# Attention of a hybrid block: all four head pairs of a token tile at once, in quarters and column halves of the array

## The reference, cut to what matters

```python
def swa_sink_attention(q, k, v, sinks, cos, sin):
    ...
    s = jnp.einsum('bnqhgd,bnkhd->bnhgqk', q, kb) * (ATT_HEAD_DIM ** -0.5)   # kb: chunk n-1 and chunk n
    s = jnp.where(valid, s, finfo.min)                                      # chunk 0 has none before it
    pr = softmax(concatenate([s, sink], axis=-1))[..., :-1]
    o = jnp.einsum('bnhgqk,bnkhd->bnqhgd', pr, vb)
...
o_b = swa_sink_attention(...)
merged = concatenate([sigmoid(gate_a) * o_a, sigmoid(gate_b) * o_b])
x = x + merged @ w_out[i]
```

## Time and profile before

| | us |
|---|---|
| median of 3 runs | 1765.84 |
| lowest and highest | 1765.23, 1767.95 |
| the profiled execution | 1764.62 |
| its span, first to last instruction | 1762.9 |
| TensorE busy | 1734.0 |
| DVE busy | 1088.1 |
| ACT busy | 905.7 |

### The profile page before, as it was taken

One profiled execution on the slowest core, in us unless ns is written; L12 is line 12 of the kernel. 1 busy time (PEld: TensorE's weight loads), 2 busy tenths in 40 slices (PEclk: granted clock), 3 DMA queues, 4 the chain that ended last, 5 costly groups with the idle time before them and its releaser, 6 DMA issues.

```text
span 1762.9 us, 22796 instructions
## 1 busy us (share of the span) xinstructions
PE 1734.0 (98%) x8277; PEld 1434.9 (81%) x8277; DVE 1088.1 (62%) x1436; ACT 905.7 (51%) x1152; POOL 20.6 (1%) x77
## 2 busy tenths in 40 slices
PE   7999999999999999999999999999999999999996
PEld 6888788888888888888888888888888888888885
DVE  6657776776757766577686454555555555555564
ACT  6556546554555545555456544444444444444453
POOL 4000000000000000000000000000000000000000
PEclk9999999999999999999999999999999999999998
DMA  6655555555655556555556666666666666665553
GB/s 220 200 171 174 148 165 177 159 166 168 190 178 158 166 168 190 178 159 166 168 181 208 186 186 190 191 191 187 193 184 192 189 190 183 193 187 186 174 187 111
DMA packets 162715, 315.32 MB, mean 179 GB/s; under 512 B 10097, under 2 KB 10418, under 8 KB 162482
## 3 DMA queue, kind: packets, MB, share of 16 engines
q1 hardware_dynamic: 161584, 312.01, 58.5%
q10 hardware_dynamic: 1026, 1.87, 0.3%
HBM read 311.74 MB, written 2.10 MB: 178 GB/s over the span
## 4 chain that ended last, share of the span: by engine, by line
PE 96%; DVE 2%; ACT 1%; issue 0%; DMA 0%; SPq 0%; DVEq 0%; ACTq 0%
PE acc L638 30%; PE acc L639 30%; PE acc L644 30%; PE turn L665 2%; PE turn L707 1%; PE turn L683 1%; PE turn L696 1%; DVE w_lo L1218 1%; ACT w_hi L894 1%; PE turn L755 0%; DMA w_raw<-in_w_in_dram 0%; PE turn L728 0%; PE turn L722 0%; DVE x_sb L1295 0%; PE turn L762 0%
## 5 line engine op out<-in xcount | busy, mean ns | idle before, releaser
L1218 DVE TENSOR_TENSOR w_lo<-w_raw,w_hi 128x1024 fp32r<-128x1024 f32 x588 | 720.1, 1225 | 612.4 <-ACT w_hi L894 608.7
L894 ACT ACTIVATE w_hi<-w_raw 128x1024 fp32r<-128x1024 f32 x588 | 623.1, 1060 | 700.8 <-PE acc L644 690.8
L638 PE MATMUL acc<-w_hi,hT_hi 128*128 128x512 f32 x1568 | 624.7, 398 | 6.5 <-ACT w_hi L894 4.0
L639 PE MATMUL acc<-w_hi,hT_lo 128*128 128x512 f32 x1568 | 612.5, 391 | 0.0
L644 PE MATMUL acc<-w_lo,hT_hi 128*128 128x512 f32 x1568 | 419.8, 389 | 0.0
L638 PEld LDWEIGHTS acc<-w_hi,hT_hi 128*128 128x128 f32 x1568 | 295.6, 189 | 68.3 <-ACT w_hi L894 4.4
L639 PEld LDWEIGHTS acc<-w_hi,hT_lo 128*128 128x128 f32 x1568 | 295.8, 189 | 59.9 <-issue 0.4
L644 PEld LDWEIGHTS acc<-w_lo,hT_hi 128*128 128x128 f32 x1568 | 294.3, 188 | 61.7
L638 PE MATMUL acc<-w_hi,mT_hi 128*128 128x512 f32 x512 | 205.5, 401 | 0.0
L639 PE MATMUL acc<-w_hi,mT_lo 128*128 128x512 f32 x512 | 199.7, 390 | 0.0
L644 PE MATMUL acc<-w_lo,mT_hi 128*128 128x512 f32 x512 | 137.3, 390 | 0.0
(11 more groups left out here) (209 smaller groups left out, 898.7 us busy)
## 6 DMA issues: line engine op xcount, KB each, us to landing
w_raw<-in_w_in_dram SPq DMA_DIRECT2D x232, 512.0 KB, 3.7
w_raw<-in_w_up_dram SPq DMA_DIRECT2D x128, 512.0 KB, 3.7
w_raw<-in_w_down_dram SPq DMA_DIRECT2D x128, 512.0 KB, 3.9
w_raw<-in_w_out_dram SPq DMA_DIRECT2D x64, 512.0 KB, 4.5
w_raw<-in_w_ple_gate_dram SPq DMA_DIRECT2D x32, 512.0 KB, 3.9
x_sb<-in_x_dram SPq DMA_DIRECT2D x8, 256.0 KB, 7.8
w_raw<-in_w_ple_proj_dram SPq DMA_DIRECT2D x4, 512.0 KB, 3.9
out_dram<-x_sb SPq DMA_DIRECT2D x3, 512.0 KB, 4.7
```

Of the source, the lines that this page charges most:

```text
L638: pe.matmul(a, hi[:, k, t, :], w_hi[:, s, kk, :], start=first and kk == 0, stop=False)
L639: pe.matmul(a, lo[:, k, t, :], w_hi[:, s, kk, :], start=False, stop=False)
L894: act.activation(w_hi[:, n % W_SLOTS], w_raw[:, n % RAW_SLOTS], ACT.Copy)\
L1218: dve.tensor_tensor(w_lo[:, n % W_SLOTS], w_raw[:, n % RAW_SLOTS], w_hi[:, n % W_SLOTS].bitcast(F32), ALU.subtract).then_inc(w_lo_ready, 1)
```

## The change

The attention of a group goes in two steps, one for each token tile, with all four pairs (8 heads) in each.

- **Scores** (a = 4 and a = 16): 16 matmuls of 128 columns, each on 64 rows (one head of the pair, `hs`) and 64 columns of the array (one chunk of 64 queries, `qs`), so that four matmuls in a row go to the four quarters. The two heads write to two banks (0 and 1). The keys stand in `kTd` unpadded, on both halves of the partitions, and each quarter takes 128 of them.
- **Softmax**: the maximum over all pairs in one go (`parts_of`: for t=0 the first 64 queries have 64 keys, all others 128); the exponentials in four steps, one for each pair, into one tile `pr` with room for 128 keys and the sink, whose exponential ACT writes beside them (16 further instructions a group). A new DVE stage, `weights_normed`, sums, inverts and multiplies, in two halves g, and the transposes wait for it (`pn_ready`).
- **Transposes of the weights**: 4 for each t and g, 16 a group, where there were 24.
- **Values**: the stationary operand is now a 64-column slice of `vv`, the weights stream, and the result is transposed already: for t=0 two matmuls of 512 columns, one to each column half of the array (one head of each pair), for t=1 four of 256 columns. `vv` has a third part with the values of chunks mixed as the third chunk of queries needs them. `weighted_values(j, 0)` stands directly behind the scores of t=1 (a = 16), `weighted_values(j, 1)` at a = 28.
- **Gating**: TensorE transposes the gate (8 transposes at a = 31) in place of the gated result, and DVE multiplies.
- **Once at the start**: 8 transposes of the keys in place of 16; ACT copies half of the values a second time; some clearing by GpSimd is gone.

The attention of a group ends at a = 33, where it ended at a = 44.

```diff
-            kTp = mb("kTp", [P, 4, 2, TT * P])
-            vaug = mb("vaug", [P, TT, 4, HD + 1])
+            kTd = mb("kTd", [P, 4, 5 * CHUNK])
+            vv = mb("vv", [P, 3, 4, HD])
...
-            pr0 = mb("pr0", [P, 2, P])
-            pr1 = mb("pr1", [P, 2, 2 * P])
-            pT = mb("pT", [P, 4, P])
-            oa = mb("oa", [P, TT, 8, HD + 1])
+            pr = mb("pr", [P, 4, 2, P + 1])
+            pT = mb("pT", [P, 2, 4, P])
+            oaT = mb("oaT", [P, 4, TT, P])
...
+        for t in range(TT):
+            use(("kT", t), t, kTd_out, t + 1)
...
-            for u in range(8):
-                use(("score", j, u), 0, pr_ready, 8 * j + u + 1)
-                use(("pT", j, u), 1, pT_out, 8 * j + u + 1)
-                use(("pv", j, u), 1, pv_out, 8 * j + u + 1)
             for t in range(TT):
-                use(("amT", j, t), t, moA_ready, 2 * j + t + 1)
+                for hh in range(2):
+                    use(("score", j, t, hh), hh, pr_ready, 4 * (2 * j + t + 1))
+                for g in range(2):
+                    use(("pT", j, t, g), g, pT_out, 2 * (2 * j + t) + g + 1)
+            use(("pv", j, 1), 0, pv_out, 2 * j + 2)
+            for t in range(TT):
+                use(("gbT", j, t), t, am_ready, 2 * j + t + 1)
...
+                if hp == 0:
+                    use(("pv", j, 0), 2, pv_out, 2 * j + 1)
...
+        SCORES, PV1, ATT_END = (4, 16), 28, 31
...
-            def scores(j, u, t, pair):
-                name = ("score", j, u)
-                if u == 0:
+            def scores(j, t):
+                if t == 0:
                     pe.wait_ge(qaT_out, 2 * (j + 1))
-                    pe.wait_ge(kTp_out, 4)
+                    pe.wait_ge(kTd_out, 2)
+                for hh in range(2):
+                    signal, value = bank_free(("score", j, t, hh))
+                    pe.wait_ge(signal, value)
+                late = kTd[:, j, P:5 * CHUNK].rearrange("p (s c) -> p s c", c=CHUNK)[:, 0:3:2, :]
+                keys = (kTd[:, j, 0:P],) * 2 if t == 0 else (kTd[:, j, P:2 * P], late)
+                for pair in range(4):
+                    for c in range(2):
+                        for hh in range(2):
+                            name, hs = ("score", j, t, hh), slice(hh * HD, (hh + 1) * HD)
+                            qs = slice(c * CHUNK, (c + 1) * CHUNK)
+                            out_ = bank(name)[qs, pair * P:(pair + 1) * P]
+                            if t and c:
+                                out_ = out_.rearrange("p (s c) -> p s c", c=CHUNK)
+                            mm = pe.matmul(out_, qT[hs, pair, t, qs], keys[c][hs], start=True, stop=True,
+                                           skip_group_check=True)
+                            if pair == 3 and c == 1:
+                                mm.then_inc(full(name), 1)
+            def weights_turn(j, t, g):
+                name = ("pT", j, t, g)
+                pe.wait_ge(pn_ready, 2 * (2 * j + t) + g + 1)
...
-                k0, nk = keys_of(t)
-                mm = pe.matmul(bank(name)[:, 0:2 * nk].rearrange("p (v k) -> p v k", v=2),
-                               qT[:, pair, t, :], kTp[:, j, :, k0:k0 + nk], start=True, stop=True)
+                for i in range(4):
+                    hh, pair = i // 2, 2 * g + i % 2
+                    mm = pe.transpose(bank(name)[:, i * P:(i + 1) * P], pr[:, pair, hh, 0:P], ident[:])
                 mm.then_inc(full(name), 1)
-            def weights_turn(j, u, t):
-                name = ("pT", j, u)
-                pe.wait_ge(pr_ready, 8 * j + u + 1)
+            def weighted_values(j, t):
+                name = ("pv", j, t)
+                pe.wait_ge(pT_out, 2 * (2 * j + t + 1))
                 signal, value = bank_free(name)
                 pe.wait_ge(signal, value)
...
-            def weighted_values(j, u, t):
...
+                parts_ = ((0, slice(0, P)),) if t == 0 else ((V_MIXED, slice(0, CHUNK)), (V_LATE, slice(CHUNK, P)))
+                for v, qs in parts_:
+                    for hh in range(2):
+                        mm = pe.matmul(four(bank(name)[hh * HD:(hh + 1) * HD, :])[:, :, qs], vv[:, v, j, :],
+                                       pT[:, hh, :, qs], start=True, stop=True, skip_group_check=True)
                 mm.then_inc(full(name), 1)
...
-                    for i in range(4):
-                        t, half = divmod(i, 2)
+                    for t in range(TT):
                         pe.wait_ge(k_rotated, t + 1)
-                        src = (gate if t == 0 else eg)[:].rearrange("p a b -> p (a b)")
-                        turn(("kT", i), lambda q: src[:, (4 * half + q) * P:(4 * half + q + 1) * P])
+                        turn(("kT", t), lambda i: gate[:, t, i * P:(i + 1) * P])
...
-                    for u in range(8):
-                        t, pair = divmod(u, 4)
-                        if a == UNIT * u + 4:
-                            scores(j, u, t, pair)
-                        if a == UNIT * u + 7:
-                            weights_turn(j, u, t)
-                        if a == UNIT * u + 9:
-                            weighted_values(j, u, t)
-                    if a == ATT_END + 4:
-                        for t in range(TT):
-                            pe.wait_ge(am_ready, 2 * j + t + 1)
-                            turn(("amT", j, t), lambda i: sgb[:, t, i * P:(i + 1) * P])
+                    for t in range(TT):
+                        if a == SCORES[t]:
+                            scores(j, t)
+                            if t == 1:
+                                weighted_values(j, 0)
+                        for g in range(2):
+                            if a == SCORES[t] + 7 + 2 * g:
+                                weights_turn(j, t, g)
+                    if a == PV1:
+                        weighted_values(j, 1)
+                    if a == ATT_END:
+                        for t in range(TT):
+                            pe.wait_ge(gb_sig, 2 * j + t + 1)
+                            turn(("gbT", j, t), lambda i: sgb[:, t, i * P:(i + 1) * P])
...
-            def exponentials(j, u, t, pair):
...
+            def exponentials(j, t, pair):
+                if pair == 0:
                     for hh in range(2):
...
+                        act.wait_ge(full(("score", j, t, hh)), nth(("score", j, t, hh)))
+                    act.wait_ge(nm_ready, 2 * j + t + 1)
+                    act.wait_ge(pr_cleared, j + 1)
+                    if j or t:
+                        act.wait_ge(pT_out, 2 * (2 * j + t))
+                for hh in range(2):
+                    head = t * 8 + 2 * pair + hh
+                    act.activation(pr[:, pair, hh, P:P + 1],
+                                   sink_bc[:, 8 * j + 2 * pair + hh:8 * j + 2 * pair + hh + 1],
+                                   ACT.Exp, bias=asc[:, NM + head:NM + head + 1])
+                    src = bank(("score", j, t, hh))
+                    for rows_, keys in parts_of(t):
+                        ins = act.activation(pr[rows_, pair, hh, 0:keys], src[rows_, pair * P:pair * P + keys], ACT.Exp,
+                                             scale=HD ** -0.5, bias=asc[rows_, NM + head:NM + head + 1])
                 ins.then_inc(pr_ready, 1)
...
-                    for u in range(8):
-                        if a == UNIT * u + 5:
-                            exponentials(j, u, *divmod(u, 4))
+                    for t in range(TT):
+                        for pair in range(4):
+                            if a == SCORES[t] + 2 + pair:
+                                exponentials(j, t, pair)
                     if a == ATT_END + 1:
...
+                        for t in range(TT):
+                            act.wait_ge(am_ready, 2 * j + t + 1)
+                            act.activation(mT_hi[:, 4:8, t, :], four(sgb[:, t]), ACT.Copy).then_inc(moA_hi, 1)
...
-            def score_max(j, u, t, pair):
...
+            def score_max(j, t):
+                for hh in range(2):
+                    name = ("score", j, t, hh)
+                    dve.wait_ge(full(name), nth(name))
+                    for rows_, keys in parts_of(t):
+                        chain(dve.tensor_reduce(asc[rows_, MX + hh:MX + 8:2], four(bank(name)[:])[rows_, :, 0:keys],
+                                                AX_X, ALU.max))
+                if j == 0 and t == 0:
                     dve.wait_ge(sinks_landed, 16)
...
-                dve.tensor_scalar(asc[:, NM + 8 * t + head:NM + 8 * t + head + 2], asc[:, MX:MX + 2], -1.0, None,
+                chain(dve.scalar_tensor_tensor(out=asc[:, MX:MX + 8], in0=asc[:, MX:MX + 8], scalar=HD ** -0.5,
+                                               in1=sink_bc[:, 8 * j:8 * j + 8], op0=ALU.mult, op1=ALU.max))
+                dve.tensor_scalar(asc[:, NM + 8 * t:NM + 8 * t + 8], asc[:, MX:MX + 8], -1.0, None,
                                   ALU.mult).then_inc(nm_ready, 1)
```

(47 more changed lines are left out.)

125 lines of the change are left out of this document (22 added, 103 removed).

## The result

The changed kernel takes 1737.74 us (median of 4 runs, 1736.98 to 1737.94) against 1765.66 for the kernel before (4 runs, 1765.23 to 1767.95). The ratio is 0.984, with a 95% interval of 0.9829 to 0.9852, so the change gains 27.9 us where the forecast had 30.2.

The account below looks back on a forecast made before the run. TensorE, busy 98% of the span, sets the pace. 25.6 us of attention, 0.8 at the start and 3.8 of stall make 30.2: profiled 1764.62 becomes 1734.4, median forecast 1735.6 us, range 1731 to 1746.

Parts of the forecast that it names:

- Four abreast: TensorE's score matmuls run in all four array quarters at once, 0.11 us per pass of 128 columns; chance 0.66.
- the slowest rival: Score passes run one after another, each of 256 with an exposed weight load of at most 0.055 us: 1777.9 us; chance 0.03.
- The visit at 0.37 us: Entering and leaving array tiles on TensorE costs 0.37 us a visit, 4.4 us for twelve; the least sure term.
- Change of shape from scores to values: At a = 16 on TensorE, going from score tiles to value tiles within one visit costs 0.14 us.
- The chunks: TensorE from L644 to L644: a = 4 3.97 us, a = 16 4.99, a = 28 3.97 apart from the recurrence's transposes.
- What is removed and added: TensorE's attention work per group: 13.0 us removed, 6.65 added, 6.4 less, 25.6 in four groups.
- Keys at the start: At the kernel's start TensorE does 8 transposes fewer at 0.105 us each, 0.8 us gained.
- The stall: In group 0 TensorE's wait for DVE's L1375, with the slow clock after it, goes away: 3.8 us gained.
- The waits at nothing: Added waits, such as transposes for `weights_normed` behind work on DVE and ACT, cost TensorE nothing.
- The rival of new waits: Lumps on DVE and ACT make TensorE wait, 3.8 us each: once 1739.4 us, once a group 1750.8; chance 0.10.
- the forecast's own sign: TensorE would show no idle time in the four groups.
- its other sign: TensorE's granted clock would be 1.00 in the four groups.

Follow-up runs that it names:

- b_early: The kernel before with every attention unit started one chunk earlier, nothing else; 1787.95 us, ratio 1.012 to the kernel before.
- o_quarter: The changed kernel with the 16 score matmuls ordered one array quarter at a time (head, then query chunk, then pair); 1747.74 us in one run.
- o_rows: The changed kernel with the 16 score matmuls ordered with query chunk outermost, so neighbours are the two row halves; 1740.40 us in one run.
- o_cols: The changed kernel with the 16 score matmuls ordered with head outermost, so neighbours are the two column halves; 1739.86 us in one run.
- pv_merged: The changed kernel with the values of t=1 moved from a=28 to a=40, directly behind the recurrence's 64-column tiles; 1735.83 us, ratio 0.9826 to the kernel before.

## Why the prediction was right, step by step

- **Four abreast**: right. The passes cost 0.109 us for 0.11, so no weight load is exposed as the slowest rival had it. The quarters' rows run independently, each with its own bank; whether they would with one bank for both was not tried.
- **The visit at 0.37 us**: right on the whole, though not one number. Alone it is 4.01 - 2.72 - 8 x 0.109 = 0.42; beside transposes 0.29; inside another visit nothing. Change of shape from scores to values: 4.99 - 4.01 - 8 x 0.109 = 0.11 for 0.14.
- **The chunks**: 4.01 for 3.97, 4.99 for 4.99, 4.36 where 3.97 and the recurrence's transposes, 3.21 - 2.72 = 0.49 by themselves, would make 4.46.
- **What is removed and added**: after, a group has 1.29 + 2.27 + 1.15 + 1.85 = 6.56 us, forecast 6.65. Chunk by chunk the attention gains 25.7 in four groups, forecast 25.6, but this close only by luck. The forecast priced every piece of the kernel before as if it stood alone; beside other small work it is cheaper (two value matmuls beside four transposes of `za` cost 3.59 - 3.21 = 0.38 for 0.47), so a group loses 12.7 us and not 13.0, 1.3 us less in four groups. The small waits around units 6 and 7 in groups 1 to 3, which the forecast didn't have, were 1.0 us and are gone too.
- **Keys at the start**: 0.9 for 0.8.
- **The stall**: 3.8 gained, as forecast. That og set it off is right. That unit 7 had no margin in any group was not seen; the forecast didn't hang on it. That the slow clock came with the wait, 1.8 of the 3.8 us, was read from one execution and taken as sure; b_early shows that it is not.
- **The waits at nothing**: the one step that failed. The terms above, 25.7, 0.9 and 3.8, make 30.3 before rounding. Of that, 2.4 us went to the wait for `za`. The text counted ACT's exponentials per step (some 2 us beside a split of 1.06 in 2.72) and took the buffers as the cover. The buffers cover the splits only: `za`, on the same engine, has a consumer one chunk away, and 2.0 + 1.06 is already above 2.72. The rival of new waits named a lump on DVE or ACT that makes TensorE wait once, or once a group. That happened at small size, 1.6 us once and 0.2 to 0.3 us three times. By the forecast's own sign, no idle time of TensorE in the four groups, this is where it was wrong; its other sign there held, for there was no fall of the granted clock, which is 1.00 in the window of 282.73 to 287.53 (the column behind the engines):

```profile
282.73:287.53 4.80, 3.41 (x18) 2.57 (x17) 3.19 (x5) 4.67 (x12) 0.00 (x0) 1.00 0.45 131
```

The price of 3.8 us that the rival put on each wait was that of an idle time of 2.0 us with the slow clock behind it. The wait of 1.39 us cost 1.6 us, less than half of that.

- **The rest**: the difference of the profiled executions is 27.6 = 30.3 - 2.4 - 1.0 + 0.7. The 1.0 is the start of the kernel, with the transposes of x, and the 0.7 lies in a few late chunks with nothing beside them. No edit explains either, and both lie within what single runs of one kernel show: the first chunk takes 4.78 us in one profiled execution of the changed kernel and 3.82 in the other.

## What to carry to other kernels

Small matmuls that use quarters of the array cost the time of the fullest quarter, if the code goes round the quarters; then put them into visits that exist already, since the entry and the way back are paid once. When work for an engine is bundled, look for every consumer behind it in its list and at its distance, not only at the stream whose buffers are deep: here 2.4 us of 30 were lost to a copy that stood last in its step, and one moved block of lines brought them back. When a forecast removes small pieces, price each beside its neighbours, not alone.

## What the runs showed of the hardware

- Matmuls to different 64x64 quarters start 7 ns apart and run fully abreast, rows and columns alike, with a bank for each row half; a quarter takes a new fp32 pass of 128 columns every 109 ns, and after the first pass of a visit the next one comes 160 ns later.
- A pass that waits for its part of the array holds back later ones only when some four wait for the same part: in o_quarter, o_rows, o_cols and pv_merged the next part's first pass starts with three still to come. Whether weight loads or matmuls fill that place was not separated.
- Idle times of TensorE of 1.39 us (changed kernel), 2.59 and 3.12 us (b_early) left the granted clock at 1.00; a clock of 0.50 followed one of 1.99 us and one of 2.57 us (b_early).
